# A two-block transformer kernel: block one's attention regrouped from 16 softmax units into 12, and the transposes of q moved behind the next chunk

## The reference

```python
sc = einsum('bgrqd,bgqnld->bgrqnl', qb, kg) * scale      # selected branch
p = masked_softmax(sc, ok)
o_slc = einsum('bgrqm,bgqmd->bgrqd', p, vg)
sc = einsum('bgrqd,bgkd->bgrqk', qb, kwb) * scale        # window branch
pw = masked_softmax(sc, okw)
o_win = einsum('bgrqk,bgkd->bgrqd', pw, vwb)
return gb[..., 0:1] * o_cmp + gb[..., 1:2] * o_slc + gb[..., 2:3] * o_win
```

## Time and profile before

| | us |
|---|---|
| median of 3 runs | 829.66 (828.75 to 830.13) |
| the profiled execution | 829.05 |
| its span | 827.3 |
| PE busy | 814.5 (98%) |
| DVE busy | 587.9 (71%) |
| ACT busy | 483.9 (58%) |
| POOL busy | 30.4 (4%) |

### The profile page before, as it was taken

How to read it: one execution, slowest core, us unless ns; L and a number is a source line. 1 busy time by engine, 2 the same in 40 slices (tenths; PEclk the granted TensorE clock), 3 DMA queues, 4 the chain that set the end, 5 groups by cost and what they waited for, 6 DMA issues and landing times.

```text
span 827.3 us, 12364 instructions
## 1 busy us (share of the span) xinstructions
PE 814.5 (98%) x5045; PEld 711.9 (86%) x5045; DVE 587.9 (71%) x767; ACT 483.9 (58%) x733; POOL 30.4 (4%) x46
## 2 busy tenths in 40 slices
PE   9999999999999999999999999999999999999996
PEld 8887987888899998988888888888788888888885
DVE  5684597988785676798777877868877656554655
ACT  5563587879666353667566656537665545554551
POOL 1103000000000000000000000020110000000000
PEclk9999999999999999999999999999999999999998
DMA  8445541414143657355555555475343554555441
GB/s 323 144 137 220 190 171 54 167 51 167 51 167 138 243 188 290 109 182 184 206 193 189 173 204 198 154 282 200 127 180 151 204 204 158 199 204 204 157 149 51
DMA packets 22360, 144.02 MB, mean 174 GB/s; under 512 B 2592, under 2 KB 3104, under 8 KB 7968
## 3 DMA queue, kind: packets, MB, share of 16 engines
q1 hardware_dynamic: 20880, 137.92, 46.8%
q10 hardware_dynamic: 1424, 5.31, 1.7%
HBM read 142.17 MB, written 1.05 MB: 173 GB/s over the span
## 4 chain that ended last, share of the span: by engine, by line
PE 86%; DVE 6%; ACT 4%; DMA 2%; issue 1%; POOL 1%; SPq 0%; DVEq 0%; POOLq 0%; ACTq 0%
PE PS L1657 19%; PE PS L1661 10%; PE PS L1710 8%; PE PS L1709 8%; PE PS L1713 8%; PE PS L1644 7%; PE PS L1645 6%; PE PS L1649 6%; DMA RAW<-in_w_stream 2%; DVE WL L1017 2%; PE PS L1804 1%; PE PS L1752 1%; PE PS L1781 1%; PE PS L1673 1%; PE PS L1968 1%
## 5 line engine op out<-in xcount | busy, mean ns | idle before, releaser
L1017 DVE TENSOR_TENSOR WL<-RAW,WH 128x2048 fp32r<-128x2048 f32 (+2 forms) x128 | 285.2, 2229 | 56.7 <-ACT WH L608 56.7
L608 ACT ACTIVATE WH<-RAW 128x2048 fp32r<-128x2048 f32 (+2 forms) x128 | 238.8, 1868 | 74.2 <-DMA RAW<-in_w_stream 54.8
L1432 DVE TENSOR_TENSOR HLS<-PS,HLS 128x512 f32<-128x512 f32 x46 | 31.7, 690 | 95.5 <-ACT HLS L924 95.5
L1657 PE MATMUL PS<-CHL,WH 128*128 128x512 f32 x368 | 92.0, 392 | 0.0
L1644 PE MATMUL PS<-BHL,WH 128*126 128x256 f32 (+2 forms) x344 | 85.8, 288 | 0.7 <-ACT TI L777 0.7
L1657 PE MATMUL PS<-BHL,WH 128*128 128x512 f32 x336 | 84.0, 392 | 0.0
L1645 PE MATMUL PS<-BHL,WH 128*126 128x256 f32 (+2 forms) x344 | 83.7, 282 | 0.0
L924 ACT ACTIVATE HLS<-PS 128x512 f32<-128x512 f32 x46 | 27.5, 597 | 95.2 <-PE PS L1661 91.0
L1657 PEld LDWEIGHTS PS<-CHL,WH 128*128 128x128 f32 x368 | 66.8, 189 | 12.3
L1657 PEld LDWEIGHTS PS<-BHL,WH 128*128 128x128 f32 x336 | 61.0, 189 | 11.2
L1710 PE MATMUL PS<-WH,AL 128*128 128x512 f32 x176 | 68.8, 391 | 0.0
(11 more groups left out here) (306 smaller groups left out, 1366.9 us busy)
## 6 DMA issues: line engine op xcount, KB each, us to landing
RAW<-in_w_stream SPq DMA_DIRECT2D x108, 1024.0 KB, 4.8
RAW<-in_w_stream SPq DMA_DIRECT2D x11, 1008.0 KB, 5.4
RAW<-in_w_stream SPq DMA_DIRECT2D x8, 704.0 KB, 4.1
WF<-in_w_stream SPq DMA_DIRECT2D x2, 1024.0 KB, 4.9
LN<-in_ln ACTq DMA_DIRECT2D x2, 1024.0 KB, 5.7
WF<-in_w_stream SPq DMA_DIRECT2D x4, 294.0 KB, 3.4
X<-in_x SPq DMA_DIRECT2D x2, 512.0 KB, 4.1
RAW<-in_w_stream SPq DMA_DIRECT2D x2, 512.0 KB, 7.6
```

Source lines behind the costliest of these rows:

```text
L608: eng.activation(WH[:, c % NSLOT, 0:CHUNKS[c][2]], raw(c), ACT.Copy).then_inc(w_hi, 1)
L1017: eng.tensor_tensor(WL[:, c % NSLOT, 0:CHUNKS[c][2]], raw(c), f32(WH[:, c % NSLOT, 0:CHUNKS[c][2]]), ALU.subtract).then_inc(w_lo, 1)
L1432: eng.tensor_tensor(HLS[:, n % 4, :, :], PS[:, bank:bank + 2, 0:TOK], HLS[:, n % 4, :, :], ALU.add)\
L1657: eng.matmul(PS[:, bank, :], wh, HL[:, k, :, :].rearrange("p a t -> p (a t)"), start=(k == 0), stop=False)
```

## The change

Block one's attention is done in 12 units instead of 16. Each group has three: query tile 0 with both branches together (2 x 128 keys, so the same 1024 scores per partition as a unit of query tile 1), and query tile 1 with branch 0 and with branch 1. They start at windows 4, 5, 7, 9, 10, 12, 14, 15, 16, 17, 19 and 20; the steps at w + 1, w + 2 and w + 3 stay at those distances, so the transposes are at 6, 7, 9, 11, 12, 14, 16, 17, 18, 19, 21, 22 and the values at 7, 8, 10, 12, 13, 15, 17, 18, 19, 20, 22, 23. A unit of query tile 0 has four score matmuls over 256 columns, one mask and one maximum over 1024 elements, eight exponentials of 128 (each has its own maximum and sum), eight transposes, and copies on both ACT and DVE. No unit's exponentials stand among the evictions of an `ri` chunk any more.

`q_transposes(0)` goes behind `q` 3 (with its result in banks 4 and 5 instead of 2 and 3), its copy to `w1` 0 behind the split of that chunk; `q_transposes(1)` goes behind `rnn` 0, its copy to `rnn` 1. The wait of `w1` 0 on the first copy is taken away; the matmul into bank 4 at window 0 waits for it instead.

```diff
-NU = 16
-U0 = 4
+NU = 12
+UNIT_WINDOWS = (4, 5, 7, 9, 10, 12, 14, 15, 16, 17, 19, 20)
-def n_tile1(u):
-    return sum(1 for x in range(u + 1) if (x >> 1) & 1)
+def unit_of(u):
+    g, n = divmod(u, 3)
+    return g, int(n > 0), max(n - 1, 0)
+def unit_at(w):
+    return UNIT_WINDOWS.index(w) if w in UNIT_WINDOWS else None
...
-        QT_BANKS = (2, 6)
+        QT_BANKS = (4, 6)
...
-                nk = P * (qt + 1)
+                parts = 1 if unit_of(u)[1] else 2
+                nk = TOK // parts
                 for i in range(4):
-                    r = 2 * (i % 2) + i // 2
-                    last = eng.activation(...)
+                    for part in range(parts):
+                        last = eng.activation(...)
                 last.then_inc(exp_done, 1)
...
             def o_first(v):
                 g, qt = v >> 1, v & 1
-                eng.wait_ge(pv_done, 2 * v + 2)
+                eng.wait_ge(pv_done, 3 * g + 2 * qt + 1)
...
-                if 0 <= w - U0 - 2 < NU:
-                    unit_pt(w - U0 - 2)
-                if 0 <= w - U0 - 3 < NU and (w - U0 - 3) % 2:
-                    o_first((w - U0 - 3) // 2)
+                u = unit_at(w - 2)
+                if u is not None:
+                    unit_pt(u)
+                u = unit_at(w - 3)
+                if u is not None and u % 3 != 1:
+                    o_first(2 * (u // 3) + u % 3 // 2)
...
                     for m, t in enumerate(gate_order(i)):
-                        if m == RG_TILES[i] - 2 and 0 <= c - W0 - U0 < NU:
-                            unit_exp(c - W0 - U0)
                         bank = wait_mb(eng, c, m)
...
-                eng.wait_ge(t_done, NU)
+                eng.wait_ge(t_done, NU - 1)
...
+                for r in range(4):
+                    keys = KT[rows, br, g, :] if qt else KT[rows, :, g, 0:P]
+                    last = eng.matmul(...)
...
                 if kind == "q" and i % 2:
                     n = i // 2
-                    if n == 1:
-                        q_copy(0)
...
                 if kind == "w1":
+                    if i == 0:
+                        q_copy(0)
...
-                if kind == "rnn" and i == 0:
+                if kind == "rnn" and i == 1:
                     q_copy(1)
...
-                if kind == "q" and i == 2:
+                if kind == "q" and i == 3:
                     q_transposes(0)
-                if kind == "w1" and i == 1:
+                if kind == "rnn" and i == 0:
                     q_transposes(1)
...
-                    eng.wait_ge(gate_ready, 1)
+                    eng.wait_ge(qkt_copied, 1)
```

More of the change, by code:

```diff
@@ L992, in _ @@
                     eng.activation(SC[:, :, :, :], SC[:, :, :, :], ACT.Exp).then_inc(sc_exp, 1)
-                if 0 <= c - W0 - U0 < NU and CHUNKS[c][0] != "ri":
-                    unit_exp(c - W0 - U0)
+                u = unit_at(c - W0)
+                if u is not None:
+                    unit_exp(u)
                 side(c)
@@ L1159, in window @@
                     ins.then_inc(pc_ready, 1)
-                if 0 <= w - U0 - 2 < NU:
-                    unit_pt(w - U0 - 2)
-                if 0 <= w - U0 - 3 < NU and (w - U0 - 3) % 2:
-                    o_second((w - U0 - 3) // 2)
+                u = unit_at(w - 2)
+                if u is not None:
+                    unit_pt(u)
+                u = unit_at(w - 3)
+                if u is not None and u % 3 != 1:
+                    o_second(2 * (u // 3) + u % 3 // 2)
             def side(c):
@@ L1763, in unit_qk @@
                     eng.wait_ge(exp_done, u)
-                def head_pair(r, nk):
+                for r in range(4):
                     h = 4 * g + r
-                    o = 64 * (h % 2)
-                    return QT[o:o + 64, h // 2, P * qt:P * qt + P], KT[o:o + 64, br, g, 0:nk]
-                scores(2, qt, head_pair).then_inc(qk_done, 1)
+                    rows = slice(64 * (h % 2), 64 * (h % 2) + 64)
+                    keys = KT[rows, br, g, :] if qt else KT[rows, :, g, 0:P]
+                    out = PS[:, 2 + r % 2, TOK * (r // 2):TOK * (r // 2) + TOK]
+                    last = eng.matmul(out if qt else out.rearrange("p (e k) -> p e k", e=2), QT[rows, h // 2, P * qt:P * qt + P], keys,
+                                      start=(r < 2), stop=(r >= 2), skip_group_check=True)
+                last.then_inc(qk_done, 1)
             def unit_t(u):
-                qt = (u >> 1) & 1
                 eng.wait_ge(p_ready, u + 1)
@@ L1776, in unit_t @@
                     eng.wait_ge(pt0_copied, u)
-                    if n_tile1(u - 1):
-                        eng.wait_ge(pt1_copied, n_tile1(u - 1))
-                for kt in range(qt + 1):
+                    eng.wait_ge(pt1_copied, u)
+                for part in range(2):
                     for i in range(4):
-                        last = eng.transpose(PS[:, 4 + kt, P * i:P * i + P], sm(u)[:, i, P * kt:P * kt + P], ident)
+                        last = eng.transpose(PS[:, 4 + part, P * i:P * i + P], sm(u)[:, i, P * part:P * part + P], ident)
                 last.then_inc(t_done, 1)
             def unit_pv(u):
-                g, qt, br = u >> 2, (u >> 1) & 1, u & 1
-                v = u >> 1
+                g, qt, br = unit_of(u)
+                v = 2 * g + qt
                 bank = 6 + v % 2
@@ L1799, in unit_pv @@
                 eng.wait_ge(pt0_copied, u + 1)
-                if qt:
-                    eng.wait_ge(pt1_copied, n_tile1(u))
-                for kt in range(qt + 1):
+                eng.wait_ge(pt1_copied, u + 1)
+                for part in range(2):
+                    key_tile, branch = (part, br) if qt else (0, part)
                     for b in range(2):
-                        last = eng.matmul(PS[64 * b:64 * b + 64, bank, 0:256], V[:, kt, br, HD * g:HD * g + HD],
-                                          PT[:, u % 2, kt, 2 * b:2 * b + 2, :].rearrange("p r q -> p (r q)"),
-                                          start=False, stop=(br == 1 and kt == qt), skip_group_check=True)
+                        last = eng.matmul(PS[64 * b:64 * b + 64, bank, 0:256], V[:, key_tile, branch, HD * g:HD * g + HD],
+                                          PT[:, u % 2, part, 2 * b:2 * b + 2, :].rearrange("p r q -> p (r q)"),
+                                          start=False, stop=(part == 1 and (br == 1 or not qt)), skip_group_check=True)
                 last.then_inc(pv_done, 1)
@@ L2221, in _ @@
             for c in range(NCH):
[L2222 to L2223 removed]
+                u = unit_at(c - W0)
+                if u is not None:
+                    unit_qk(u)
                 main(c)
```

90 lines of the change are left out of this document (46 added, 44 removed).

## The result

| | before | after |
|---|---|---|
| median of 9 runs each, on one chip | 829.62 us (828.75 to 833.42) | 831.96 us (830.75 to 835.28) |
| ratio, 95% interval | | 1.0023 (1.0012 to 1.0034) |
| profiled execution, and its span | 829.05, 827.3 us | 831.35, 829.5 us |
| mean clock granted to PE in the profiled execution | 0.997 | 0.994 |

The changed kernel is slower by 0.23%, just more than the 0.2% that a measurement of this kernel tells from no change. The forecast was 832.0 us. The nine runs have a mean granted clock of 0.987 to 0.995 (median 0.993); 23 runs of the kernel before, taken later beside q_only, have 0.994 to 0.999 (median 0.997). By an estimate from the medians, 0.004 / 0.5 of 830 us, the changed kernel spends some 6.6 us more at half clock, in most of its runs and not only in the profiled one.

A forecast was written before the change was run, and what follows sets the result against it. PE, busy 98% of the span, was taken as the bound. The terms -2.1 + 2.5 - 3.2 + 3.35 gave +0.5 us on 829.66, plus 1.5 to 3.0 for clock falls: forecast 832.0 us, range 828.4 to 834.6.

The forecast's parts named there:

- Step 1: At q's transposes: PE's waits for the normed halves go when the transposes move later; -2.1 us.
- The low part of `rnn` 0: DVE makes it behind the second `QN`; ends about 77.4, PE asks at 77.7; 0 and up to 0.3 us.
- Step 2: First unit, window 5: doubled mask, maximum and exponentials make PE's next scores wait about 2.8 us; +2.5 us.
- Step 3: Fewer and merged units: PE's scores and values take less, with fewer waits and turns between kinds of matmul; -3.2 us.
- The narrow place: Window 17: scores wait for window 16's exponentials, ending about 200.3, PE arriving 200.6; 0, up to +0.8 us.
- Step 4: Last unit: its values stand behind `ri` 4, so `ao` 0 waits for ACT and DVE to take them out; +3.35 us.
- The clock: PE idles of 2.8 us (window 5) and 3.35 us (`ao` 0) likely drop the clock to half; 1.5 us per fall.
- My own reading of the end of the kernel: After the kernel's last matmuls the clock fell to half; so an idle of some 2.2 us was taken as enough.
- My sign for a fall: A page slice with PEclk under 9 near 112 or 255, and 256-column matmuls over 0.2 us apart instead of 0.12.
- Rival 2: The clock holds through both gaps, at window 5 and `ao` 0: 830.2 us (829.4 to 831.1); chance 0.29.
- Rival 3: The first unit's chain isn't late at window 5 and no clock falls there: 827.7 us; chance 0.10.
- Rival 4: ACT is late at window 17, or `rnn` 0's low part is, plus longer clock falls: 834.5 us; chance 0.18.

The follow-up runs named there:

- q_only: The kernel before with only the q part of the change (both q transposes a chunk later); 828.39 us, ratio 0.9979 to the kernel before.
- units_only: The changed kernel with the q part turned back, so 12 units but q's transposes where they were; 834.21 us, ratio 1.0050 to the kernel before.
- last_early: The changed kernel with a unit at window 11 in place of 20, so the last values stand ahead of `ri` 4; 830.52 us, ratio 1.0001 to the kernel before.
- tile1_first: The changed kernel with each group's two query tile 1 units first and the merged tile 0 unit last; 829.93 us, ratio 1.0004 to the kernel before.
- both_18: The changed kernel with units at windows 6, 11 and 18 in place of 5, 16 and 20; 833.35 us, ratio 1.0037 to the kernel before.
- before_again: The kernel before, unchanged, run and profiled a second time; 830.43 us, ratio 1.0003.
- keep_clock2: The changed kernel with 13 unused 128x512 matmuls added on PE in the gap ahead of `ao` 0; 830.83 us, ratio 1.0008 to the kernel before.
- both: The changed kernel with units at windows 6 and 11 in place of 5 and 20; 831.35 us, ratio 1.0015 to the kernel before.
- cs_twice: The kernel before with the matmuls of the compressed scores done twice into the same places; 839.45 us, ratio 1.0112 to the kernel before.
- keep_clock: The changed kernel with 26 unused 128x512 matmuls added on PE ahead of `ao` 0; 833.76 us, ratio 1.0050 to the kernel before.
- second_late: The changed kernel with its second unit at window 6 in place of 5; 832.97 us, ratio 1.0041 to the kernel before.
- tile1_early: The changed kernel with tile 1 units first in each group, and units at windows 4, 5, 7-12, 14, 15, 17, 19; 832.63 us, ratio 1.0030 to the kernel before.

## Why the prediction was right

- **Step 1, -2.1.** Right. `rnn` 0 began at 75.56 (75.8 reckoned), and q_only and units_only each give 1.8 to 2.2 us. The low part of `rnn` 0, the next thing that could have been late, wasn't.
- **Step 2, +2.5.** The chain is right to 0.3 us: mask 1.23, maximum 1.23, second scores at 111.82 (112.1 reckoned). The wait was 1.37 us instead of 2.8 in the profiled execution, since the clock had fallen in `ri` 0 and PE came later; where it hadn't (last_early), the wait was 2.77. tile1_first shows the cause.
- **Step 3, -3.2.** Right: `ri` 4 began at 247.40 (247.5). The narrow place, window 17, had no wait (scores at 200.57, reckoned 200.6; the exponentials end at 200.4, reckoned 200.3). How narrow it was is shown by last_early, where the same place cost 0.81.
- **Step 4, +3.35.** Right: gap 3.27, `ao` 0 at 254.67 (254.8), in the order of ACT's work that was written down.
- **The clock, +1.5.** Right in size and partly in place. The fall at `ao` 0 cost 1.47 us where it stood, 1.26 of it left at 310 us. The Trainium skill's advice (TensorE: Matmul & The Clock Gate, Why this matters for your kernels) against idle gaps of PE holds there: with the gap filled, the fall was gone. My own reading of the end of the kernel, that an idle of some 2.2 us is enough, isn't a rule: waits of 2.77 and 3.27 us had a fall, one of 2.81 us in both_18 had none. At window 5 no fall came in the profiled execution, where the wait was 1.4 us; with the full 2.77 us it came in last_early and cost 2.86, just above my 0.8 to 2.8. My sum had the 2.8 us wait as certain and one fall for both gaps; in truth the two compensate in part. That just one of the two gaps cost a fall in the profiled execution is luck, and the medians agree to 0.04 us by luck too. What I had missed is the fall behind the compressed scores, for which there is no gap. It raised no cost here, because the 1.5 us that it adds to `ri` 0 is covered by the wait of window 5. My sign for a fall, a slice of the page under 9, couldn't have shown it: the page of before_again is 9 in all 40 slices with a fall of 3.4 us in it, so the row of nines didn't show either that the clock of the kernel before never falls.
- **What I had not in the sum** is +0.57 us behind 310 us, by waits behind DVE (`X`, `RQK`) that differ from kernel to kernel and between two profiles of the same kernel: `RQK` from no wait to 0.9 us, `MG` from no wait to 1.37. With it the span is 2.2 us longer, where the forecast had 2.0 (0.5 + 1.5); without it 1.6.
- **The rivals.** Rival 2 (the clock holds) is refuted at `ao` 0 by the windows with the clock and by keep_clock2, and keep_clock2, 0.0008 above the kernel before (0.7 us), is near the 0.5 us that it named. Rival 3 (the first unit isn't late) is refuted by the waits. Rival 4 (ACT later at window 17) didn't happen in the changed kernel, but is what last_early, both and tile1_first paid.

## What to carry to other kernels

When PE is busy for 98% of the span, a merge that takes 3.2 us of matmuls away can still lose: look at which engine's chain PE meets at the first and at the last of the merged steps, since a doubled step on DVE and ACT has no earlier step to hide behind there, and the last one has the next stage behind it. Moving a step away from such a place helps only if the late engine has room there; three of my kernels only moved the wait from window 5 to window 7, where ACT's table loads stood. A change of independent parts should be measured part by part: here one part gained 0.2% and the other lost more.

## What the runs showed of the hardware

- The clock granted to PE fell to 0.50 at the end of 16 back-to-back f32 matmuls of 128x32 (32 records, 3.5 us) in 7 of 13 profiles, PE being busy all the time. With twice as many, in one profile, the low stretch began among them, 4.1 us before their end, and lasted 6.8 us.
- The length of a low stretch wasn't fixed: 3.4 us in most, 6.8 us in last_early, both and cs_twice, some 10 us in keep_clock. Where no wait followed, one of 3.4 us cost 1.47 us (`ao` 0), and two of 6.8 us cost 2.86 (last_early) and 2.77 (both). A fall right ahead of a wait cost next to nothing (second scores at 111.82 with it, 111.80 without).
- Waits of PE of 1.3 to 1.5 us never had a fall behind them, nor had one of 1.85 us (both_18). Of eight waits of 2.6 to 3.4 us, seven had (after, units_only, second_late and tile1_first at `ao` 0; last_early at window 5; both at window 7; tile1_early in `ri` 1), and one of 2.81 us (both_18 at window 7) hadn't. Why one held isn't known.
